# Second expert layer: outputs summed in PSUM by TensorE, and the 32 lightest experts taken four to a pass

## The reference, cut to what matters

```
scores = sigmoid(h @ w_router)
_, idx = top_k(scores + e_bias, TOP_K)                 # TOP_K = 8 of 64 experts
wts = take_along_axis(scores, idx); wts = wts / wts.sum(-1) * ROUTE_SCALE
...                                                    # tokens gathered by expert
a = silu(xb @ w_gate[e]) * (xb @ w_up[e])              # xb: tokens x 1024, w: 1024 x 256
yb = a @ w_down[e]                                     # 256 x 1024
routed = zeros(n_tok, d).at[slot_tok].add(yb * slot_w) # weighted sum over a token's 8 experts
y = routed + (silu(h @ s_gate) * (h @ s_up)) @ s_down
```

## Time and profile before

| | |
|---|---|
| median of 3 runs | 3846.54 us (3842.4 to 3852.73) |
| the profiled execution, its time | 3851.95 us |
| its span | 3850.3 us |
| granted TensorE clock, mean | 0.941 |
| TensorE busy | 85% of the span |
| DMA, mean over the span | 232 GB/s |

### The profile page before, as it was taken

How to read it: one execution, slowest core, us unless ns; L and a number is a source line. 1 busy time by engine, 2 the same in 40 slices (tenths; PEclk the granted TensorE clock), 3 DMA queues, 4 the chain that set the end, 5 groups by cost and what they waited for, 6 DMA issues and landing times.

```text
span 3850.3 us, 40161 instructions
## 1 busy us (share of the span) xinstructions
PE 3283.4 (85%) x13994; PEld 2225.9 (58%) x13994; DVE 1409.8 (37%) x3100; ACT 536.5 (14%) x1051; POOL 502.2 (13%) x527
## 2 busy tenths in 40 slices
PE   3799897998999997889998978989876989777776
PEld 2678775887877886778564433444434675222223
DVE  7556614555013564574263322222213052111112
ACT  1210014100011002100031111111111031111111
POOL 0010103001000000000213111211112012111111
PEclk9899998999999999999998999999988999898988
DMA  7467631774425771465200589999992219999995
GB/s 286 175 240 282 228 132 66 273 274 169 151 108 189 294 267 66 158 255 221 77 30 4 208 282 389 383 375 373 361 324 78 77 44 333 393 394 386 389 386 163
DMA packets 143079, 893.62 MB, mean 232 GB/s; under 512 B 20416, under 2 KB 23616, under 8 KB 45376
## 3 DMA queue, kind: packets, MB, share of 16 engines
q1 hardware_dynamic: 94528, 675.32, 44.6%
q0 software_dynamic: 46912, 213.95, 18.0%
q10 hardware_dynamic: 1472, 2.18, 0.2%
HBM read 853.62 MB, written 57.67 MB: 237 GB/s over the span
## 4 chain that ended last, share of the span: by engine, by line
PE 65%; DMA 19%; DVE 8%; issue 5%; ACT 1%; POOL 1%; SPq 1%; POOLq 0%; DVEq 0%; ACTq 0%
PE ps L670 14%; DMA ring<-stream_in 13%; PE ps L951 12%; PE ps L934 9%; PE ps L707 8%; PE ps L1193 8%; PE ps L1213 5%; DMA moe_out<-arena,slot_out 3%; DMA arena<-mod_stream_in 2%; PE ps L1161 1%; PE ps L696 1%; DVE arena L1621 1%; PE ps L1128 1%; DVE YS L1723 1%; PE ps L682 1%
## 5 line engine op out<-in xcount | busy, mean ns | idle before, releaser
L1193 PE MATMUL ps<-ring,arena 128*64 128x512 f32 (+1 forms) x2112 | 639.7, 621 | 98.6 <-DMA ring<-stream_in 98.6
L1193 PEld LDWEIGHTS ps<-ring,arena 128*64 128x64 f32 (+1 forms) x2112 | 234.3, 159 | 443.6 <-issue 440.5
L1621 DVE SCALAR_TENSOR_TENSOR arena<-arena,cond 128x512 f32<-128x512 f32 x630 | 447.6, 748 | 72.4 <-DMA arena<-mod_stream_in 62.4
L934 PE MATMUL ps<-H,ring 128*128 128x256 f32 x2048 | 455.4, 384 | 14.3 <-ACT H L1331 14.3
L951 PE MATMUL ps<-arena,ring 128*128 128x256 f32 x2048 | 448.1, 381 | 4.3 <-DVE arena L1883 4.3
L934 PEld LDWEIGHTS ps<-H,ring 128*128 128x128 f32 x2048 | 392.0, 193 | 69.4 <-issue 15.7
L1213 PE MATMUL ps<-ring,arena 128*64 128x512 f32 (+1 forms) x1056 | 348.3, 667 | 95.3 <-issue 82.6
L951 PEld LDWEIGHTS ps<-arena,ring 128*128 128x128 f32 x2048 | 390.4, 191 | 57.9 <-issue 5.0
L1213 PEld LDWEIGHTS ps<-ring,arena 128*64 128x64 f32 (+1 forms) x1056 | 123.8, 169 | 312.4 <-issue 295.4
L2088 DVE TENSOR_TENSOR arena<-arena,ps 128x256 f32<-128x256 f32 x86 | 36.2, 421 | 649.4 <-ACT arena L1527 649.4
L2400 POOL DMA_INDIRECT moe_out<-arena,slot_out x86 | 137.3, 1597 | 1021.9 <-DVE arena L2139 843.5
(11 more groups left out here) (247 smaller groups left out, 3086.5 us busy)
## 6 DMA issues: line engine op xcount, KB each, us to landing
ring<-stream_in SPq DMA_DIRECT2D x618, 1024.0 KB
arena<-mod_stream_in POOLq DMA_DIRECT2D x120, 1024.0 KB, 5.1
arena<-mod_stream_in SPq DMA_DIRECT2D x12, 1024.0 KB, 6.9
YS<-mod_stream_in SPq DMA_DIRECT2D x12, 1024.0 KB, 4.8
moe_out<-zeros POOLq DMA_DIRECT2D x16, 256.0 KB, 3.5
arena<-moe_out POOLq DMA_DIRECT2D x6, 512.0 KB, 4.5
moe_in<-YS POOLq DMA_DIRECT2D x1, 2048.0 KB, 7.6
moe_out<-arena POOLq DMA_DIRECT2D x1, 2048.0 KB, 8.1
```

Source lines behind the costliest of these rows:

```text
L934: m = mm(out[:, i * T:(i + 1) * T], w[:, c * 256 + i * P:c * 256 + i * P + P], h_lat[c], start=(c == 0), stop=(c == DC - 1))
L1193: m = mm(out[at, :], e_xt[:, k % 2, 4 * part + c, at], w[:, c * TC:(c + 1) * TC], start=(part == c == 0), stop=(part == 1 and c == 3))
L1621: ins = stt(acc, w, x, acc, MUL, ADD)
```

## The change

In layer 1 the passes are 28: ranks 0 to 7 alone, ranks 8 to 31 in 12 pairs, and ranks 32 to 63 four to a pass in 8 passes with 32 slots each (called fours below). They alternate: one, two, four, two, and so on; the last three are four, four, one. The weighted sum over experts is made by TensorE: DVE builds `t_spread` (slots x 256 tokens, the weight where slot and token meet), and four matmuls a pass (`summed_rows`) add `t_spread^T @ e_y` into PSUM banks 0 to 3, which hold the 256 x 1024 sums all the time and get the shared expert's output first. The scatters, the store and load of `moe_out` and the lane of zeros go, in layer 1. The other work of a pass shares banks 4 to 7. `slot_out` is no longer made there. In both layers PE and POOL skip the spare loop by one branch when there is nothing in it; ACT and DVE still go through it, and in layer 1 it has 15 turns in place of 12, as more experts have few slots.

```diff
+        if l == 0:
+            order["moe", l] = Phase([0, 1, 2, 3, 4, 6, 7], 3 * EXPERTS, fills=n)
+            order["moe_turn", l] = Phase(list(range(8)), 0)
+        else:
+            order["moe", l] = Passes([5, 5, 7, 7, 4, 6, 6], 3 * EXPERTS, n, summed_order(n))
+            order["moe_sum", l] = Phase([0, 1, 2, 3], 0)
+            order["moe_turn", l] = Phase([4, 5, 6, 7, 0, 1, 2, 3], 0)
...
+def summed_order(n):
+    order = [(SLOT, k) for k in range(4)] + [(ROWS_T + half, k) for k in range(2) for half in range(2)] + [(HIDDEN, 0)]
+    for k in range(n):
+        order += [(HIDDEN_T, k), (ROWS_T, k + 2), (HIDDEN, k + 1), (SLOT, k + 4), (ROWS_T + 1, k + 2), (OUTPUT, k), (OUTPUT + 1, k)]
+    return [(i, k) for i, k in order if k < n]
...
     second = []
-    for r in range(4):
-        second += solo(r)
-    for r in range(8, EXPERTS, 2):
-        second += pair(r)
-    for r in range(4, 8):
-        second += solo(r)
+    for r in range(7):
+        second += solo(r) + pair(8 + 2 * r) + [Round(tuple(range(32 + 4 * r, 36 + 4 * r)))]
+        if 22 + 2 * r < 32:
+            second += pair(22 + 2 * r)
+    second += [Round((60, 61, 62, 63))] + solo(7)
...
-                    freed = [piece_used[(ph.first + j) % SLOTS] for j in plan_.freed[k, part]]
-                    if k == part == 0:
-                        freed = [piece_used[(ph.first - 1) % SLOTS]]
-                    return views, iter(freed)
-
-                def freeing(m, freed):
-
-                    piece = next(freed, None)
-                    if piece is not None:
-                        m.then_inc(piece, 1)
+                    done.extend(piece_used[(ph.first + j) % SLOTS] for j in plan_.freed[k, part])
+                    return views
+
+                done = [piece_used[(ph.first - 1) % SLOTS]]
+
+                def freeing(m):
+
+                    if done:
+                        m.then_inc(done.pop(0), 1)
...
+                def down(k, half):
+                    if half == 0:
+                        views = weights(k, 2)
+                        wait_drained(pe, ph, HIDDEN_T, k)
+                    else:
+                        views = [ring[:, (ph.first + plan_.order.index((r, 2))) % SLOTS, :] for r in rounds[k].ranks]
+                    out, full = bank(ph, OUTPUT + half, k)
+                    for c in range(2):
+                        for w, (r, at) in zip(views, rounds[k].lanes):
+                            m = mm(out[at, :], e_ht[:, c, at], w[:, c * D + half * 512:c * D + (half + 1) * 512],
+                                   start=(c == 0), stop=(c == 1))
+                            if c == 0:
+                                freeing(m)
+                    m.then_inc(full, 1)
+
+                def summed_rows(k, half):
+
+                    if k < 0:
+                        return
+                    if half == 0:
+                        pe.wait_ge(spread_ready, k + 1)
+                        wait_drained(pe, ph, OUTPUT, k)
+                    else:
+                        wait_drained(pe, ph, OUTPUT + 1, k)
+                    for tb in range(nb):
+                        m = mm(ps[:, 2 * tb + half, :], t_spread[:, k % 2, tb * P:(tb + 1) * P], e_y[:, k % 2, half * 512:(half + 1) * 512],
+                               start=False, stop=(k == len(rounds) - 1))
+                        if k == len(rounds) - 1:
+                            m.then_inc(filled[2 * tb + half], 1)
+                    if half and k < len(rounds) - 1:
+                        m.then_inc(summed, 1)
...
+                else:
+                    for i in range(2 * nb):
+                        out, _ = bank(PLAN["moe_sum", l], i)
+                        tb, at = i // 2, (i % 2) * 512
+                        for c in range(2):
+                            m = mm(out, sh_h[:, c, tb * P:(tb + 1) * P], w[:, c * D + at:c * D + at + 512], start=(c == 0), stop=False)
+                            if i == c == 0:
+                                m.then_inc(used, 1)
+                    for k in range(2):
+                        rows_turned(k, 0)
+                        rows_turned(k, 1)
+                    gate_up(0)
+                    for k in range(len(rounds)):
+                        hidden_turned(k)
+                        rows_turned(k + 2, 0)
+                        gate_up(k + 1)
+                        slots(k + 4)
+                        rows_turned(k + 2, 1)
+                        down(k, 0)
+                        summed_rows(k - 1, 0)
+                        down(k, 1)
+                        summed_rows(k - 1, 1)
...
                 with pe.If(n_spare > 0):
                     spare_slots(0, 0)
-                spare_turns(pe, l, n_spare, spare_block)
+                    spare_turns(pe, l, n_spare, spare_block)
+                if l:
+                    summed_rows(len(rounds) - 1, 0)
+                    summed_rows(len(rounds) - 1, 1)
...
+                        wait_past(act, summed, k - 1)
+                        drain(ph, OUTPUT, e_y[:, k % 2, 0:512], whole, turn=k)
...
                 spare_turns(act, l, n_spare, spare_block)
+                if l:
+                    for tb in range(nb):
+                        drain(PLAN["moe_sum", l], 2 * tb, e_acc[:, tb, 0:512], whole)
...
+                def spread(k):
+
+                    wait_past(dve, summed, k - 1)
+                    ts(t_spread[:, k % 2, :], t_number, slot_rec[:, k % RECORDS, 0:1], slot_rec[:, k % RECORDS, 1:2], ALU.is_equal, MUL)\
+                        .then_inc(spread_ready, 1)
...
+                        spread(k)
+                        gated(k + 1)
+                        records(k + 4)
+                        one_hot(k + 5)
+                        rows_turned(k + 2)
+                        wait_past(dve, summed, k - 1)
+                        drain(ph, OUTPUT + 1, e_y[:, k % 2, 512:D], turn=k)
...
                 spare_turns(dve, l, n_spare, spare_block, spare_pick)
-                dve.wait_ge(lane_loaded, 16 * (l + 1))
+                if l:
+                    for tb in range(nb):
+                        drain(PLAN["moe_sum", l], 2 * tb + 1, e_acc[:, tb, 512:D])
+                    return
...
                 with pool.If(n_spare > 0):
                     spare_rows(0, 0)
-                spare_turns(pool, l, n_spare, spare_block, spare_pick)
+                    spare_turns(pool, l, n_spare, spare_block, spare_pick)
+                if l:
+                    return
```

More of the change, by code:

```diff
@@ L180, with __init__, fill @@
 LANE_B = TC + P
+class Passes(Phase):
+    def __init__(self, banks, pieces, fills, order):
+        super().__init__(banks, pieces, fills=fills)
+        self.nth = {at: [banks[i] for i, _ in order[:n + 1]].count(banks[at[0]]) for n, at in enumerate(order)}
+    def fill(self, k, turn=0):
+        b = self.banks[k]
+        return b, self.base[b] + self.nth[k, turn]
+def summed_order(n):
[3 more added lines that the diff above has]
+    return [(i, k) for i, k in order if k < n]
 class Round:
@@ L475, in build @@
         h2_rows = lane_rows = YS[:, :].rearrange("p (a n) -> p a n", a=4)
+        t_number, t_spread, sp_spread = YS[:, 0:T], *(YS[:, i * T:(i + 2) * T].rearrange("p (a t) -> p a t", a=2) for i in (1, 3))
+        sp_y = YS[:, D + TC:3 * D + TC].rearrange("p (a n) -> p a n", a=2)
         mla_scale = float((MLA_NOPE + MLA_ROPE) ** -0.5)
@@ L1156, in rows_turned @@
                     pe.wait_ge(gathered[k % 2], 16 * ((before + k) // 2 + 1))
[L1157 to L1162, removed]
+                    out, full = bank(ph, ROWS_T + half, k)
+                    for c in range(4):
+                        at = (4 * half + c) * P
+                        m = nc.tensor.transpose(out[:, c * P:(c + 1) * P], e_x[:, k % 2, at:at + P], ident)
+                    m.then_inc(full, 1)
                 def weights(k, part):
@@ L1189, in gate_up @@
                     for part in range(2):
-                        views, freed = weights(k, part)
+                        views = weights(k, part)
                         for c in range(4):
@@ L1239, in moe @@
                 n_spare = spares(pe, l)
+                at = SPARE_AT[l]
                 def spare_slots(i, b):
                     pe.wait_ge(spare["onehot"][l], i + 1)
-                    products(ps[:, 2, 0:2], [(sp_hot[:, tb, :], sp_vals[b][:, tb, :]) for tb in range(nb)], spare["slots"][l])
+                    products(ps[:, at.slots, 0:2], [(sp_hot[:, tb, :], sp_vals[b][:, tb, :]) for tb in range(nb)],
+                             spare["slots"][l])
                 def spare_block(j, b, n):
@@ L2070, in records @@
                     token = slot_rec[:, k % RECORDS, 0:1]
[L2071 to L2074 removed]
+                    if l == 0 and rounds[k].pair:
+                        stt(slot_out[:, at], token, V("slot", 3), V("slot", 4), ADD, ALU.min)
+                    elif l == 0:
```

(7 more changed lines are left out.)

216 lines of the change are left out of this document (127 added, 89 removed).

## The result

The changed kernel takes **3822.6 us** (median of 5 runs, 3820.5 to 3826.0) against 3846.54 before. The ratio of the two is **0.9934, interval 0.9921 to 0.9947**: faster by 0.7%, 24 us, a third of the forecast 67. That lies above the range. The profiled execution took 3826.0, its span is 3824.3.

The account below looks back on a forecast made before the run. The prediction took layer 1's expert stage as bound by transfers; -50 us (its stream), -10.8 (the end) and -7.0 (layer 0) sum to -67.8, giving 3784 profiled, 3780 us against the median, range 3750 to 3812.

Parts of the forecast that it names:

- What bounds the kernel now: Layer 1's expert passes: transfers bound the stage, 2.55 us a weight piece, a scatter between 2.3 and 3.4 us.
- Passes after: TensorE in layer 1: 15.1 us a pass with sums, 28 passes 423 us against 421 before; fours 1.0 to 1.3.
- two at a time: Rival: a four's experts run two by two, costing TensorE 10.3 us more per four; 3807, chance 0.08.
- in turn: Rival: a four's matmuls take turns, 31 us more per four; slower, 3927, chance 0.05.
- The stream after: Layer 1's weight transfers: 490 us of pieces, 14 of gathers, 50 of gaps; last `down` near 3750, -50 us.
- neighbour: Two steps of four pieces in a row hold all 8 slots: gap 3.4 us, 10 places, 34 us; bounds 2.0 and 5.0.
- a turn: Passes of one, two, four, two: ring may fill behind a four, 1.6 us each, 5 turns, 8; bounds 0 and 4.
- The sign that I had set for a wrong stream: End of layer 1's passes: a last `down` past 3790 would prove the sum for the transfers wrong.
- The range: Whole kernel: low end 3750 from pieces of 2.45 and gaps of 2.0; high end 3812.
- the stream gains nothing: Rival: some slots always held, each step waits a full transfer; only the end and layer 0 gain; 3828, chance 0.05.
- The end after: Last `down` to TensorE's turning in layer 1: 12.2 us, not 23.0, with DVE's 15 spare turns in it; -10.8 us.
- Layer 0: End of layer 0: one branch replaces GpSimd's 16 empty spare turns between last scatter and load; -7.0 us.

Follow-up runs that it names:

- e4: The kernel before with layer 1's scatters and the waits for them left out, its routed experts missing from that layer's output: 3772.5 us, ratio 0.9795.
- e7: The changed kernel with ACT and DVE too skipping the empty spare loop by one branch: 3817.1 us, ratio 0.9914.
- e8: The changed kernel with layer 1's slots freed by the last matmul reading them, and ACT and DVE skipping the empty spare loop: 3758.9 us, ratio 0.9773.
- e9: The kernel before with only PE and POOL skipping the empty spare loop, in both layers: 3838.1 us, ratio 0.9971.
- e10: The changed kernel run once more, unaltered, for its own spread: 3826.2 us, ratio 0.9940.

## Why the prediction went wrong, by its own steps

- **What bounds the kernel now**: right. Transfers bound the stage. A piece measured without scatters (e4) is 2.57 us, the forecast's 2.55 from the queue's share; after, it is 83.4% of 580 us for 195.15 MB, 2.60. The 0.05 over 192 pieces are 10 us.
- **Passes after**: right enough. Four side by side cost 7.28 us against 7.03. A one-expert pass is 15.17 (forecast 15.1), a pair's 15.93: where matmuls onto 64 or 32 partitions stand beside the sums' 128, a group of 4 to 16 instructions takes 1.82 to 1.91 us from its start to the next group's and not 1.72, 0.1 to 0.2 more, four times a pass. By the Trainium skill's "TensorEngine Tiling (Array Packing)", Key Properties, a change of tiling mode drains TensorE; the trace agrees in kind and gives a price, but no run tests that the time is this drain. The 1.3 taken from the Trainium skill's "TensorE: Matmul & The Clock Gate", Part 3, for several tiles did not show. Both rivals on fours (two at a time, in turn) fell, the slower one with them.
- **The stream after**: this is **the step that failed**. Its mechanism was right, place by place: "all 8 slots are held", "the queue runs dry". Its sizes were not. A neighbour was put at 3.4 us, the fixed part of a store, one matmul at full clock and the issue; it is 5.0, since the data thins out over the 1.9 us before TensorE's start, and the clock has fallen by then, so the first freeing takes twice as long. That was my own upper bound. Behind a four's `down` I took 1.6 us a turn, on the ground that TensorE is the slower one there; the slots are held through `down`, sums and transposes, and it is about 3. And the last three passes, where four meets four, I counted as two more neighbours; there TensorE waits before each step of a four. In all 76 us dry before the last landing and not 50. The account from the stream's start to the last `down`: +26 dry, +13 in transfers (pieces of 2.60 and the stretches with a share of 0.9 to 1), +2 from the last landing to the last `down` (13.2 against 11): 41. The sign that I had set for a wrong stream, a last `down` past 3790, did not come, as it ended at 3787.8: that bound stood too far out. The share of 0.90 came as forecast too. The sign that did fail is the weights' rate, 349 GB/s in the steady part (156.16 MB in 447 us) and not about 365.
- **The range**: it was built from one bound at a time. The upper bound of the neighbours (5.0 each, +16), that of the turns (+12 for five of them) and pieces of 2.60 (+10) all point one way, and the first two have one cause, slots held too long, so they come together: 3780 + 38 = 3818. At the low end, my -16 for pieces of 2.45 should have read -19 for 192 pieces. That I left 0.05 for "the stream gains nothing" (3828) was too little: by the weights of the steady part (156.2 against 155.3 MB) that rival came closer than the forecast.
- **The end after**: right, 12.1 for 12.2, with DVE's loop as the cause (e7, e8). What I said would stand without it, 6.6 + 0.9, is 5.3. Turning to end was 3.2 us shorter, which I had at nothing; half of it is the norm's first matmuls, which follow the turning's start by 3.5 us and not 5.1.
- **Layer 0**: right as a step (e9: -6.8, and the 128 matmuls behind layer 1's attention start 6.5 earlier, 3115.42 against 3121.95). In after DVE's first sum starts at 2894.5, 6.7 us earlier than before, in e10 at 2892.7, 8.5 earlier. Of these 3.7 and 8.2 are left at those 128 matmuls (3118.27 and 3113.79), so what that one profile lost on the way is an execution's chance. In the head of the layer the shared expert's output into the banks takes 8.80 us, before 7.10; I had not counted these 1.7.

## What to carry to other kernels

Count the slots of a ring against the largest step that waits for all its pieces at once. If that step and the one before fill the ring, the queue stops at every such place until a slot is freed behind the wait: here 4.9 us each time. Free each piece by the last instruction that reads it, not by the next step: here that alone was worth 1.6%, more than twice what the whole change brought. And work taken off a queue is worth only what the next queue can take up: ask what the transfers that remain wait for, before multiplying the ones removed.

## What the runs showed of the hardware

- TensorE's granted clock fell from 1.00 to 0.50 in the wait of 5.67 us before 3317.24 (windows 3313 to 3321). Behind the eight waits of 4.40 to 6.78 us before a four's second part, its 32 instructions took 5.36 to 6.37 us in place of 3.64. The length of the wait alone does not tell: behind one of 3.76 us (3774.21) 16 instructions ran in 1.92 us at 1.00, and behind one of 2.51 us (3696.69) 32 took 5.34.
- At the neighbour read above the last packets of a piece came 0.7 us before the matmul that waited for it started, and the share had fallen to 0.24 by 3314.75, 2.5 us before it. From the issue on SyncE's queue to the first data were about 0.9 us.
- Four float32 matmuls onto 32 partitions each run side by side in full: the 64 instructions of a four's `gate_up` would take 7.28 us (32 in 3.64), the 16 of one expert's take 7.03.
- Where groups of matmuls onto 64 or 32 partitions alternate with groups onto 128, each group takes 0.1 to 0.2 us longer (1.82 to 1.91 us against 1.72).
